# A RetNet decoder step in hand-ordered form: hi and lo parts for the key-value and score-value products

## The reference

```python
def retention_chunk(q, k, v, s_prev, log_gamma):
    ...
    scores = jnp.einsum('bhnd,bhmd->bhnm', q, k) * decay_mask[None].astype(q.dtype)
    inner = jnp.einsum('bhnm,bhme->bhne', scores, v)
    cross = jnp.einsum('bhnd,bhde->bhne', q, s_prev.astype(q.dtype)) * cross_decay[None, :, :, None].astype(q.dtype)
    kv = jnp.einsum('bhmd,bhme->bhde', k * k_decay[None, :, :, None].astype(k.dtype), v)
    s_new = jnp.exp(log_gamma * L)[None, :, None, None] * s_prev + kv
    return inner + cross, s_new.astype(s_prev.dtype)
...
    mu = jnp.mean(of, axis=-1, keepdims=True)
    var = jnp.mean(jnp.square(of - mu), axis=-1, keepdims=True)
    o = ((of - mu) * lax.rsqrt(var + GN_EPS)).astype(h.dtype)
    return (jax.nn.silu(g) * o) @ w_out, s
```

## Time and profile before

| what | value |
|---|---|
| median of 3 runs | 1473.08 us (1473.06 to 1473.17) |
| the profiled execution, and its span | 1473.48 us, 1471.4 us |
| PE busy | 1465.5 us (100% of the span) |
| DVE, ACT busy | 778.1 us (53%), 522.2 us (35%) |
| granted PE clock, mean | 1.0 of full speed |
| the four heads | from the start to about 513 us of the span |

### The profile page before, as it was taken

How to read it: one execution, slowest core, us unless ns; L and a number is a source line. 1 busy time by engine, 2 the same in 40 slices (tenths; PEclk the granted TensorE clock), 3 DMA queues, 4 the chain that set the end, 5 groups by cost and what they waited for, 6 DMA issues and landing times.

```text
span 1471.4 us, 27541 instructions
## 1 busy us (share of the span) xinstructions
PE 1465.5 (100%) x11540; PEld 1402.9 (95%) x11540; DVE 778.1 (53%) x1047; ACT 522.2 (35%) x736; POOL 5.0 (0%) x26
## 2 busy tenths in 40 slices
PE   9999999999999999999999999999999999999998
PEld 9699879969978999999999999999999999999998
DVE  7675458358446965555552325455465555554222
ACT  5452164155136543333331323222343333333222
POOL 0000000000000000000000000000000000000000
PEclk9999999999999999999999999999999999999999
DMA  6544353462454232222222222222222232222321
GB/s 241 216 172 150 131 200 120 148 238 91 152 191 183 92 101 88 98 86 86 100 89 87 100 86 86 94 94 87 95 93 86 88 97 86 96 89 90 100 87 58
DMA packets 47743, 171.91 MB, mean 117 GB/s; under 512 B 5608, under 2 KB 6248, under 8 KB 46624
## 3 DMA queue, kind: packets, MB, share of 16 engines
q1 hardware_dynamic: 47488, 170.71, 33.6%
q0 software_dynamic: 32, 0.03, 0.0%
q10 hardware_dynamic: 144, 0.00, 0.0%
HBM read 149.39 MB, written 21.55 MB: 116 GB/s over the span
## 4 chain that ended last, share of the span: by engine, by line
issue 77%; PE 22%; DMA 0%; SPq 0%; DVE 0%; ACT 0%; POOLq 0%; POOL 0%; ACTq 0%
PE ps L405 11%; PE ps L521 5%; PE ps L575 1%; PE ps L606 1%; PE ps L602 1%; PE ps L565 1%; PE ps L599 1%; PE ps L554 1%; PE ps L501 0%; DMA w_raw<-in_w_units_dram 0%; PE ps L438 0%; PE ps L537 0%; PE ps L613 0%; SPq L303 0%; PE ps L581 0%
## 5 line engine op out<-in xcount | busy, mean ns | idle before, releaser
L856 ACT ACTIVATE w_hi<-w_raw 128x1024 fp32r<-128x1024 f32 x227 | 239.5, 1059 | 745.9 <-PE ps L405 469.9
L1148 DVE TENSOR_TENSOR w_lo<-w_raw,w_hi 128x1024 fp32r<-128x1024 f32 x227 | 276.7, 1222 | 364.1 <-ACT w_hi L856 363.9
L405 PE MATMUL ps<-h_hi,w_hi 128*128 128x264 f32 (+2 forms) x2300 | 468.0, 285 | 0.7 <-DVE h_lo L1176 0.7
L405 PE MATMUL ps<-h_lo,w_hi 128*128 128x264 f32 (+2 forms) x2300 | 465.4, 284 | 0.0
L405 PE MATMUL ps<-h_hi,w_lo 128*128 128x264 f32 (+2 forms) x2300 | 464.9, 283 | 0.0
L405 PEld LDWEIGHTS ps<-h_hi,w_hi 128*128 128x128 f32 x2300 | 355.7, 188 | 1.8 <-issue 1.0
L405 PEld LDWEIGHTS ps<-h_hi,w_lo 128*128 128x128 f32 x2300 | 355.6, 188 | 0.0
L405 PEld LDWEIGHTS ps<-h_lo,w_hi 128*128 128x128 f32 x2300 | 355.2, 188 | 0.0
L705 PE MATMUL ps<-z_hi,w_lo 128*128 128x264 f32 (+1 forms) x704 | 144.7, 283 | 0.0
L705 PE MATMUL ps<-z_hi,w_hi 128*128 128x264 f32 (+1 forms) x704 | 144.6, 283 | 0.0
L705 PE MATMUL ps<-z_lo,w_hi 128*128 128x264 f32 (+1 forms) x704 | 144.6, 283 | 0.0
(11 more groups left out here) (202 smaller groups left out, 1384.9 us busy)
## 6 DMA issues: line engine op xcount, KB each, us to landing
w_raw<-in_w_units_dram SPq DMA_DIRECT2D x227, 512.0 KB, 3.3
states<-in_state_ret_dram SPq DMA_DIRECT2D x32, 512.0 KB, 6.4
out_ret_s_dram<-states SPq DMA_DIRECT2D x32, 512.0 KB, 3.2
v_bcast<-v_scratch SPq DMA_DIRECT2D x8, 1024.0 KB, 5.7
x_res<-in_x_all_dram SPq DMA_DIRECT2D x8, 268.0 KB, 6.2
out_ret_p_dram<-tmp SPq DMA_DIRECT2D x4, 512.0 KB, 2.7
out_y_prompt_dram<-y_rows SPq DMA_DIRECT2D x4, 512.0 KB, 2.6
decay<-in_decay_dram SPq DMA_DIRECT2D x4, 287.0 KB, 4.8
```

The costliest lines, as they stand in the source:

```text
L405: out = mm(PS[:, 2 * s + half, at:at + n_col], a, b[:, lo:lo + n_col], start=first and n == 0, stop=last and n == 2)
L856: fn(WH[:, c % NS, :], RAW[:, c % NR, :], ACT.Copy).then_inc(hi_ready, 1)
L1148: tt(WL[:, c % NS, :], RAW[:, c % NR, :], WH[:, c % NS, :].bitcast(F32), ALU.subtract).then_inc(lo_ready, 1)
```

## The change

- The value rows V become VH and VL, the key rows KN become KNH and KNL, the scores PR become PRH and PRL, all `float32r`; the last 24 rows (16 tokens and 8 samples) stay `float32` (VE, PE24).
- Each product over them is three `float32r` matmuls in place of one `float32` matmul. L602, L565, L613 and L438 stay.
- ACT writes the hi parts (all four value blocks now, two before; two copies for the scores), DVE the lo parts (four value blocks, four key blocks, two pieces of the scores). PR moves into the scratch tile.
- Broadcast value rows are held for four samples; those of samples 4 to 7 come in separate DMAs, each after `update(b)` for b = 0 to 3.
- The outer products and updates of the samples' states come later in each engine's order.

```diff
                 sp.wait_ge(v_sent, 16 * h + 16)
-                for half in range(2):
-                    b = half * NB // 2
-                    sp.dma_start(VB[:, b:b + NB // 2, :], VSCR[b:b + NB // 2, :].partition_broadcast(P)).then_inc(vb_in[half], 16)
+                sp.dma_start(VB[:], VSCR[0:NB // 2, :].partition_broadcast(P)).then_inc(vb_in, 16)
...
                 for b in range(NB):
                     sp.wait_ge(s_upd, NB * h + (b + 1))
+                    if b < NB // 2:
+                        sp.dma_start(VB[:, b, :], VSCR[b + NB // 2, :].partition_broadcast(P)).then_inc(vb_next[b], 16)
                     sp.dma_start(st_out[b, h], S[:, b, :]).then_inc(s_out[b], 16)
...
-                pe.wait_ge(kn_ready, 4 * h + 4)
                 for js in ((0, 1), (2, 3, 4)):
                     for e in range(2):
                         if js[0] == 2:
                             pe.wait_ge(mid_ready, 2 * h + e + 1)
+                        else:
+                            pe.wait_ge(kn_lo, 4 * h + 2 * e + 2)
                         for j in js[:2]:
-                            out = mm(PS[:, 6 + e, :], KN[:, j, e * P:(e + 1) * P], V[:, j, :], start=j in (0, 2), stop=j == 1)
+                            kh, kl = KNH[:, j, e * P:(e + 1) * P], KNL[:, j, e * P:(e + 1) * P]
+                            for q, (k, v) in enumerate(((kh, VH), (kh, VL), (kl, VH))):
+                                out = mm(PS[:, 6 + e, :], k, v[:, j, :], start=j in (0, 2) and q == 0, stop=j == 1 and q == 2)
...
                 pe.wait_ge(p_ready, 5 * h + 5)
+                pe.wait_ge(p_hi, 2 * h + 2)
+                pe.wait_ge(p_lo, 2 * h + 2)
...
+                    def keys(j, at, c0, c1, first, last):
+                        vh, vl = VH[:, j, vt], VL[:, j, vt]
+                        for q, (v, p) in enumerate(((vh, PRH), (vh, PRL), (vl, PRH))):
+                            mm(PS[:, 2 * s + j // 2, at:at + c1 - c0], v, p[:, c0:c1], start=first and q == 0, stop=last and q == 2)
+
                     for j in range(2):
...
+                        keys(j, CUT + q0, PCOL[j] + q0 - BLK[j][0], PCOL[j + 1], j == 0, j == 1)
...
+                    for j in range(2, 4):
+                        keys(j, BLK[j][0] - CUT, PCOL[j], PCOL[j + 1], False, False)
+                    out = mm(PS[:, 2 * s + 1, 4 * P - CUT:T - CUT], VE[0:24, vt], PE24[0:24, :], start=False, stop=True)
                     out.then_inc(inner_done, 1)
...
                 for n in range(5, 7):
                     split_hi(n + NS, U_HEAD, h)
-                outer(0)
                 for e in range(2):
                     act.wait_ge(mid_done, 2 * h + e + 1)
                     fn(KM[:, e * DV:(e + 1) * DV], PS[:, 6 + e, :], ACT.Copy).then_inc(mid_ready, 1)
                 split_hi(7 + NS, U_HEAD, h)
 
-                outer(1)
                 act.wait_ge(kv_done, h + 1)
                 fn(OS[:], PS[:, 1, :], ACT.Copy).then_inc(os_ready, 1)
+                outer(0)
+                outer(1)
                 for dt in range(4):
-                    outer(dt + 2)
+                    if dt in (1, 2):
+                        outer(dt + 1)
                     act.wait_ge(inner_done, 4 * h + (dt + 1))
...
-                outer(6)
-                outer(7)
+                outer(4)
+                outer(5)
                 split_hi(8 + NS, U_HEAD, h)
+                outer(6)
                 act.wait_ge(kv_sent, 16 * h + 16)
                 for dt in range(4):
                     act.wait_ge(o_cent, 4 * h + (dt + 1))
                     fn(TMP[:, dt, 0:N_RET], O[:, dt, C_RET:], ACT.Square).then_inc(o_sq, 1)
+                outer(7)
                 split_hi(9 + NS, U_HEAD, h)
...
+                for b in range(4):
+                    dve.wait_ge(v_ready, 5 * h + b + 2)
+                    stt(VL[:, b, :], PS[:, 2 + b, :], RN[:, b:b + 1], VH[:, b, :].bitcast(F32), ALU.mult, ALU.subtract).then_inc(v_lo, 1)
+
+                def k_rest(j):
...
+                    stt(KNL[:, j, :], src, DEC[:, DEC_ROW + j:DEC_ROW + j + 1], KNH[:, j, :].bitcast(F32),
+                        ALU.mult, ALU.subtract).then_inc(kn_lo, 1)
...
-                for n in range(5, 7):
+                for n, (c0, c1) in enumerate(((C_RET, PCOL[2]), (PCOL[2], PCOL[4]))):
+                    dve.wait_ge(p_hi, 2 * h + n + 1)
+                    tt(PRL[:, c0:c1], PR[:, c0:c1], PRH[:, c0:c1].bitcast(F32), ALU.subtract).then_inc(p_lo, 1)
+                for n in range(5, 8):
                     split_lo(NS + n, U_HEAD, h)
-                update(0)
-                split_lo(NS + 7, U_HEAD, h)
...
-                for b in range(1, 5):
+                for b in range(4):
                     update(b)
...
-                update(5)
+                update(4)
...
+                update(5)
                 update(6)
+                split_lo(NS + 8, U_HEAD, h)
                 update(7)
-                split_lo(NS + 8, U_HEAD, h)
```

More of the change, by code:

```diff
@@ L52 @@
 PCOL = [0, 256, 384, 656, 800]
-PTOT = 824
 N_LATE = TP - CUT
@@ L147, in build @@
             Q, K = O[:, 0:2, :], O[:, 2:4, :]
-            V = sb("v_rows", [P, 5, DV], scope=s2)
-            KN = sb("k_rows", [P, 4, DK], scope=s2)
+            VH = sb("v_rows_hi", [P, 4, DV], F32R, scope=s2)
+            VE = sb("v_rows_end", [P, DV], scope=s2)
             KT = sb("k_tail_stack", [P, DK], F32R, scope=s2)
+            with ExitStack() as s7:
+                KNH = sb("k_rows_hi", [P, 4, DK], F32R, scope=s7)
+                KNL = sb("k_rows_lo", [P, 4, DK], F32R, scope=s7)
             G = sb("gate", [P, 4 * N_RET], scope=s2)
-            PR = sb("scores", [P, PTOT], scope=s2)
+            PRH = sb("scores_hi", [P, PCOL[4]], F32R, scope=s2)
+            PRL = sb("scores_lo", [P, PCOL[4]], F32R, scope=s2)
+            PE24 = sb("scores_end", [P, 24], scope=s2)
             with ExitStack() as s6:
@@ L178, in build @@
             sem("v_sent"), sem("kv_sent"), sem("copied"), sem("sent"))
-        vb_in = [sem(f"vb_in{half}") for half in range(2)]
+        vb_in, vb_next = sem("vb_in"), [sem(f"vb_next{b}") for b in range(NB // 2)]
         head_stored, rows_seen = sem("head_stored"), sem("rows_seen")
@@ L542, in head @@
                 for j, (m0, mn) in enumerate(BLK):
[L543 to L549, removed]
+                    if j < 3:
+                        pe.wait_ge(v_lo, 4 * h + (1, 3, 4)[j])
                     for e in range(2):
@@ L928, in head @@
                 fn(VT, PS[:, 0, 0:P], ACT.Copy, scale=RN[:, 4:5]).then_inc(v_ready, 1)
-                for b in (0, 2):
-                    act.wait_ge(v_acc, 3 * h + b + 1)
-                    fn(V[:, b, :], PS[:, 2 + b, :], ACT.Copy, scale=RN[:, b:b + 1]).then_inc(v_ready, 1)
+                for b in range(4):
+                    if b < 3:
+                        act.wait_ge(v_acc, 3 * h + b + 1)
+                    else:
+                        act.wait_ge(unit_done, U_HEAD * h + (NS + 8))
+                    fn(VH[:, b, :], PS[:, 2 + b, :], ACT.Copy, scale=RN[:, b:b + 1]).then_inc(v_ready, 1)
                 def outer(b):
-                    if b in (0, NB // 2):
-                        act.wait_ge(vb_in[b // (NB // 2)], 16 * h + 16)
+                    c = b % (NB // 2)
+                    act.wait_ge(vb_in if b == c else vb_next[c], 16 * h + 16)
                     if b >= 2:
@@ L940, in outer @@
                         at = (b % 2) * 1024 + e * DV
-                        fn(G[:, at:at + DV], VB[:, b, :], ACT.Copy, scale=KD8[:, e, b:b + 1]).then_inc(samp_kv, 1)
+                        fn(G[:, at:at + DV], VB[:, c, :], ACT.Copy, scale=KD8[:, e, b:b + 1]).then_inc(samp_kv, 1)
                 act.wait_ge(dec_in, 16 * h + 16)
@@ L946, in head @@
                     src = PS[:, (6, 6, 7, 7)[j], (j % 2) * DK:(j % 2 + 1) * DK]
-                    fn(KN[:, j, :], src, ACT.Copy, scale=DEC[:, DEC_ROW + j:DEC_ROW + j + 1]).then_inc(kn_ready, 1)
+                    fn(KNH[:, j, :], src, ACT.Copy, scale=DEC[:, DEC_ROW + j:DEC_ROW + j + 1]).then_inc(kn_ready, 1)
                 act.wait_ge(knat_done, 2 * h + 2)
@@ L954, in head @@
                 for at in (0, 32):
-                    fn(VS[at:at + 16, :], V[0:16, 4, :], ACT.Copy).then_inc(vs_hi, 1)
+                    fn(VS[at:at + 16, :], VE[0:16, :], ACT.Copy).then_inc(vs_hi, 1)
+                for n, c0, c1 in ((2, C_RET, PCOL[2]), (4, PCOL[2], PCOL[4])):
+                    act.wait_ge(p_ready, 5 * h + n)
+                    fn(PRH[:, c0:c1], PR[:, c0:c1], ACT.Copy).then_inc(p_hi, 1)
                 for n in range(5, 7):
                     split_hi(n + NS, U_HEAD, h)
-                outer(0)
                 for e in range(2):
@@ L1347, in head @@
                 dve.wait_ge(mid_ready, 2 * h + 2)
+                dve.wait_ge(p_lo, 2 * h + 2)
                 tt(KV, PS[:, 6:8, :].rearrange("p e v -> p (e v)"), KM, ALU.add).then_inc(kv_ready, 1)
-                for b in range(1, 5):
```

(1 more changed line is left out.)

42 lines of the change are left out of this document (20 added, 22 removed).

## The result

The changed kernel takes 1478.28 us (median of 7 runs, 1478.15 to 1478.42) where the kernel before, run beside it on the same chip, takes 1473.31 (7 runs, 1473.06 to 1474.5). The ratio is 1.0033, with a 95% interval of 1.0024 to 1.0043: slower by 5.0 us, and by more than the 0.2% that can be told apart. The span of the profiled execution grew from 1471.4 to 1476.4 us. The forecast was 1478.5 us.

A forecast was written before the change was run, and what follows sets the result against it. PE's own list of matmuls was taken to bound the kernel, with two helper chains turning late: 4 x (2.4 of waits - 1.06 of gain) = +5.4 us on 1473.08 gave 1478.5 us, range 1473.2 to 1484.8.

The forecast's parts named there:

- key-value product: On PE, 16 float32 passes (6.88 us) give way to 24 float32r matmuls (5.58 us): gain 1.30 us a head.
- score-value product: On PE, short float32r matmuls held by weight loads: 1.40 us in for 1.34 out a tile, 0.24 us a head lost.
- (a): Second statistic: outer(6) on ACT delays the squares 1.24 us against 0.71 of room; PE waits 0.55 us a head.
- (b): Output projection, first ZRL part: a third update on DVE makes its stretch 14.25 us; PE waits 1.68 us a head.
- (c): Gate's last product, 3.09 us behind the first ZRL part, asked for after 2.89: PE waits 0.2 us a head.
- PE's list and two chains: PE's own matmuls set the time; the ACT and DVE chains beside it, just in time before, might end too late.
- the forecast's estimate by the Trainium skill's load time: Score-value product at about 107 ns per load of 128 columns: sum 0.5 us lower over the four heads.
- The rival at the columns' rate: Score-value product: short float32r matmuls run at their columns' rate, 1.08 us a tile for 1.34; total 1473.3 us, chance 0.11.
- hand-over: Delay from DVE's result to PE's start: 0.02 us in (a), 0.05 us in (b).
- Hidden work: DVE's new lo parts (some 4 us), ACT's hi parts and four separate broadcasts, ahead of the score-value product: costed at nothing.
- The chains keep up: Rival at (a) and (b): added ACT and DVE work stays within its room, -4.2 us, 1468.8 us; chance 0.05.

The follow-up runs named there:

- e4: Kernel before with only the changed kernel's later places of outer products and updates, no split products or high and low parts: 1484.07 us.
- e3: Changed kernel with outer(6), outer(7) on ACT and update(5), update(6) on DVE moved earlier, update(7) alone behind the sums of squares: 1467.59 us.
- e6: Changed kernel with the float32r matmuls of 128 and 144 columns cut to 64 columns: 1477.93 us.
- e2: Changed kernel with update(5) on DVE moved right behind update(4), ahead of the sums for the statistics: 1473.41 us.
- e7: e3 with each tile's 24-row float32 matmul moved directly behind the 280-column float32 matmuls: 1468.71 us.
- e9: e3 with the last product of each tile over 128 rows instead of 24, the added rows zeroed: 1463.61 us.

## Why the prediction was right

By its own steps, in us a head:

| step | forecast | measured | from |
|---|---|---|---|
| key-value product | -1.30 | -1.30 | 6.14 for 7.44 |
| score-value product | +0.24 | 0.00 | 11.15 (449.57 to 460.72) for 11.15 |
| (a) second statistic | 0.55 | 0.67 | 8.84 for 8.17 |
| (b) first ZRL part | 1.68 | 1.68 | 14.25 for 12.57 |
| (c) gate's last product | 0.2 | 0.2 | 3.09 for 2.89 |
| sum | +1.34 | +1.25 | |

Four times the measured sum is 5.0 us, the growth of the span. (The forecast's own terms are rounded; they give 1.37.)

- **Bound by PE's list and two chains.** Right, and shown: e4 has the chains' cost alone (+10.8), e3 the list's gain alone (-5.7).
- **Key-value product.** Right to the hundredth; the new matmuls had rows of their own kind before.
- **Score-value product.** The mechanism was right, the size off. A third of the short matmuls takes 0.06 us and not the 0.114 that I gave all, about 0.1 us less a tile. Half of it goes back behind them, where the 280-column passes and the step after them take 0.79 + 0.33 us and not 0.95 + 0.124. The sum had no term for either, and together they make the 0.05 us by which a tile was mis-sized (2.82 for 2.81 + 0.06). A small slip: the forecast's estimate by the Trainium skill's load time should read 0.7 us lower over the four heads, not 0.5 (in each of 16 tiles six matmuls of 0.107 us for 0.114, and three of 0.113). e6 settles that the others are held by loads. The rival at the columns' rate is out. The Trainium skill, "TensorE: Matmul & The Clock Gate", section "Weight-path perf modes", whose fast load would have stood behind it, has nothing here that speaks for it: the steps stay at 0.11.
- **(a).** The 1.24 us of `outer(6)` against 0.71 of room was right (2.19 - 0.96 = 1.23). Mis-sized was the hand-over: PE starts 0.15 us behind the sums' end (474.93 against 474.78), where I had 0.02.
- **(b).** 14.25 us on DVE forecast and measured. The sum had a hand-over of 0.05 us at either end of the stretch (14.25 + 0.05 against 12.57 + 0.05, and 0.02 for the same hand-over in (a)); there are 0.15 at both (489.18 against 489.03), and they cancel in the one case as in the other. e2 takes one update out and gets 1.20 back.
- **(c).** Right. Behind each wait the first step is also 0.08 us longer, 0.80 us (489.18 to 489.98 in the changed kernel) where it was 0.72. Behind the first two the next wait takes that up, behind the third it stays.
- **Hidden work.** Right that it costs nothing: e4 without it has the same waits, and no wait among scores or value rows is in the changed kernel.
- **"The chains keep up".** Out as the changed kernel stands. e3 shows it is a matter of order alone; 1468.8 was its price, and 1467.6 was measured with the room made.

The errors of +0.24 and -0.12 a head cancelled in part, so the total within 0.2 us is partly luck; each step by itself was within 0.24 us a head.

## What to carry to other kernels

When a saving on the bound engine comes with work moved on its helpers, take the two apart: here -5.7 and +10.7 us made a small loss, and putting the moved work into idle time that was there kept the saving whole. For such a move count the idle time just ahead of each thing the bound engine asks for, never the engine's busy share: 1.2 us cost nothing ahead of the first statistic and all of it behind the sums of squares. Before a `float32` product is split in three, look at its width: it pays at 512 columns (0.70 for 0.86 us) and loses at 128 and 144.

## What the runs showed of the hardware

- Going from 128 to 24 rows and back cost 0.25 us a tile, 4.0 us in sixteen, since neither load overlapped the matmul ahead (e7's loads); the same product padded to 128 rows ran faster (e9 against e3). It isn't so for every product of fewer rows: the load of 96 rows of `v_tail_stack` starts at 447.47 in the changed kernel, ahead of its matmul at 447.70, under a matmul of 128 rows. That one is `float32r` and the 24-row one `float32`, and no run tells the two differences apart.
- In a row of short `float32r` matmuls with weights loaded anew the step is 0.11 us at 64, 128 and 144 columns. The first after a longer one steps by its own columns (0.03 us at 64, 0.06 at 128), but ahead of the 280-column passes what it saves comes back (e6).
- PE starts 0.15 us behind the end of the DVE instruction that it waits for, at all three places where it waits (the third: 492.27, behind the gate's product on DVE from 491.42 to 492.12).
